# Splitting each weight tile's residual subtraction between VectorE and GpSimd in a one-layer hybrid decoder trunk

## The reference, cut to what matters

```python
h = rmsnorm(x, mix_norm_w[l])
(hq, hf, hi, hg, dq, ..., gz, gate_logits) = jnp.split(h @ w_in[l], IN_SPLITS, axis=-1)
o_a = hgrn2_mixer(...)            # gated linear recurrence
o_b = diff_attention_mixer(...)
o_c = nsa_mixer(...)              # with compress_tokens: flat @ w1
o_d = chunk_gmlp_mixer(...)
merged = sum over b of gates[:, :, b] * (o_b @ w_branch[l, b])
x = x + merged @ w_out[l]
x = x + cross_attention(rmsnorm(x, xa_norm_w[l]), mem_n, xa_w_q[l], xa_w_kv[l], xa_w_o[l])
x = x + swiglu_ffn(rmsnorm(x, ffn_norm_w[l]), ffn_w_in[l], ffn_w_out[l])
return rmsnorm(x, final_norm_w)
```

## Time and profile before

| | |
|---|---|
| Time, median of 3 (lowest to highest) | 2071.66 us (2069.86 to 2072.21) |
| The profiled execution | 2072.21 us, span 2070.4 us |
| PE busy | 2026.4 us, 98% |
| PEld busy | 1772.2 us, 86% |
| DVE busy | 1301.8 us, 63% |
| ACT busy | 936.5 us, 45% |
| POOL busy | 7.9 us, under 1% |
| Granted TensorE clock, mean | 0.995 |

### The profile page before, as it was taken

The page is one execution under the profiler, slowest core; times in us unless marked ns, Lnnn a source line. Parts: engine busy times, 40 slices in busy tenths (PEclk is TensorE's granted clock), DMA queues, the critical chain, the costliest instruction groups (busy, mean ns, idle before and its releaser), DMA issues.

```text
span 2070.4 us, 30081 instructions
## 1 busy us (share of the span) xinstructions
PE 2026.4 (98%) x11734; PEld 1772.2 (86%) x11734; DVE 1301.8 (63%) x1528; ACT 936.5 (45%) x1126; POOL 7.9 (0%) x14
## 2 busy tenths in 40 slices
PE   7999999999999999999999999999999999999997
PEld 6788878887888888888888888888888888888886
DVE  7467776578666656677454447766666666645554
ACT  5364454555444444445434334444444444433342
POOL 0000000000000000000000000000000000000000
PEclk9999999999999999999999999999999999999998
DMA  6444455345555555555555436555555555565553
GB/s 239 143 173 163 172 198 179 133 145 215 189 183 182 183 185 190 214 185 181 194 192 181 144 114 212 203 184 193 191 183 193 191 184 192 191 225 193 192 185 121
DMA packets 53212, 378.29 MB, mean 183 GB/s; under 512 B 6160, under 2 KB 6416, under 8 KB 8464
## 3 DMA queue, kind: packets, MB, share of 16 engines
q1 hardware_dynamic: 50688, 365.71, 50.3%
q10 hardware_dynamic: 2448, 11.48, 1.4%
HBM read 372.98 MB, written 4.19 MB: 182 GB/s over the span
## 4 chain that ended last, share of the span: by engine, by line
PE 55%; issue 36%; DVE 6%; ACT 2%; DMA 0%; POOL 0%; DVEq 0%; POOLq 0%; ACTq 0%
PE acc L1288 33%; PE acc L1289 17%; DVE w_lo L735 2%; PE m L1367 1%; PE m L1696 1%; PE m L1672 1%; ACT w_hi L319 1%; ACT probs L370 0%; DVE x_weighted_split L1044 0%; DVE branch_now L740 0%; DVE norm L779 0%; PE m L1390 0%; DVE branch_gated L1097 0%; PE m L1492 0%; DVE x_split L785 0%
## 5 line engine op out<-in xcount | busy, mean ns | idle before, releaser
L1288 PE MATMUL acc<-x_split,w_hi 128*128 128x512 f32 x3344 | 1179.0, 397 | 10.2 <-DVE x_split L785 6.3
L735 DVE TENSOR_TENSOR w_lo<-raw,w_hi 128x2048 fp32r<-128x2048 f32 x346 | 792.5, 2291 | 351.4 <-ACT w_hi L319 347.3
L1289 PE MATMUL acc<-x_split,w_lo 128*128 128x256 f32 x3344 | 937.7, 280 | 0.0
L1288 PEld LDWEIGHTS acc<-x_split,w_hi 128*128 128x128 f32 x3344 | 628.1, 188 | 156.7 <-DVE x_split L785 6.9
L319 ACT ACTIVATE w_hi<-raw 128x2048 fp32r<-128x2048 f32 x346 | 661.2, 1911 | 99.5 <-DMA raw<-in_w_fo 87.5
L1289 PEld LDWEIGHTS acc<-x_split,w_lo 128*128 128x128 f32 x3344 | 633.0, 189 | 0.5 <-issue 0.2
L329 ACT ACTIVATE evac_half<-acc 128x256 f32<-128x256 f32 x358 | 136.4, 383 | 891.0 <-PE acc L1289 891.0
L1288 PE MATMUL acc<-mem_split,w_hi 128*128 128x512 f32 x768 | 267.9, 393 | 0.7 <-DVE mem_split L1171 0.7
L1288 PE MATMUL acc<-ffn_split,w_hi 128*128 128x512 f32 x704 | 244.1, 391 | 0.0
L1289 PE MATMUL acc<-mem_split,w_lo 128*128 128x256 f32 x768 | 214.9, 280 | 0.0
L1289 PE MATMUL acc<-ffn_split,w_lo 128*128 128x256 f32 x704 | 197.1, 280 | 0.0
(11 more groups left out here) (293 smaller groups left out, 1199.1 us busy)
## 6 DMA issues: line engine op xcount, KB each, us to landing
raw<-in_w_fi SPq DMA_DIRECT2D x88, 1024.0 KB, 4.9
raw<-in_w_gate_b SPq DMA_DIRECT2D x60, 1024.0 KB, 4.9
raw<-in_w_start SPq DMA_DIRECT2D x54, 1024.0 KB, 4.9
raw<-in_w_fo SPq DMA_DIRECT2D x44, 1024.0 KB, 4.9
raw<-in_w_kv SPq DMA_DIRECT2D x32, 1024.0 KB, 4.9
raw<-in_w_gate_a SPq DMA_DIRECT2D x16, 1024.0 KB, 4.9
raw<-in_w_out SPq DMA_DIRECT2D x16, 1024.0 KB, 4.9
raw<-in_w_q SPq DMA_DIRECT2D x16, 1024.0 KB, 4.9
```

The lines of the kernel that those rows point to most:

```text
L735: dve.tensor_tensor(w_lo(n), RAW[:, n[2] % RAWS], w_hi(n).bitcast(F32), ALU.subtract).then_inc(lo_done, 1)
L1288: pe.matmul(acc[bank][:], w_hi(n)[:, c], x, start=start, stop=False)
L1289: return pe.matmul(acc[bank][:, 0:S], w_lo(n)[:, c], x[:, 0:S], start=False, stop=stop)
```

## The change

A tile's subtraction is parted by blocks. DVE does the first `b` of the 16 blocks and POOL the other 16 - `b`, each as one instruction, and PE waits for both. A function picks `b` by the tile's number. Inside loops the tile's number is not known (`None`) and `b` is 10. POOL gets a list of its own, with all 346 tiles and the eight powers between them.

| Tiles | b (DVE) | POOL's blocks |
|---|---|---|
| 0, 1 | 6 | 10 |
| 2 to 5 | 5 | 11 |
| 6 to 15 | 10 | 6 |
| 16 to 35 | 4 | 12 |
| 36 to 53: `cmp` | 8 | 8 |
| 36 to 53: `mix` | 6 | 10 |
| 54 to 69 | 4 | 12 |
| 70 to 74 | 6 | 10 |
| 75 to 345 | 10 | 6 |

```diff
+def dve_blocks(t):
+    if t is not None and t <= 5:
+        return 6 if t < 2 else 5
+    if t is not None and WIDE1 <= t < WIDE1 + 5:
+        return 6
+    if t is None or not WIDE0 <= t < WIDE1:
+        return 10
+    if t < GA0 and START[t][0] == "cmp":
+        return 8
+    return 6 if 36 <= t < GA0 else 4
...
-        lo_done = sem("lo_done")
+        lo_dve = sem("lo_dve")
+        lo_pool = sem("lo_pool")
...
@@ block.gpsimd
+            def lo(n):
+                rs, b = n[2] % RAWS, dve_blocks(tile_no(n))
+                pool.wait_ge(hi_done, val(n, 1))
+                pool.tensor_tensor(w_lo(n)[:, b:TB], RAW[:, rs, b:TB], w_hi(n)[:, b:TB].bitcast(F32),
+                                   ALU.subtract).then_inc(lo_pool, 1)
...
             pool.wait_ge(sem("ones"), 2)
+            lo(at(0))
+            lo(at(1))
             scale("n0", NT)
-            scale("hg", 2 * H)
-            scale("da", 2 * H)
-            for name in ("ln", "nm", "n1", "n2", "n3"):
-                scale(name, NT)
+            for t in range(WIDE1):
+                lo(at(t + AHEAD))
+                if t == 37:
+                    scale("hg", 2 * H)
+                if t == 51:
+                    scale("da", 2 * H)
+                if t == 64:
+                    scale("ln", NT)
+            for t in range(WIDE1, WIDE1 + 4):
+                lo(at(t + AHEAD))
+            steps("gb")
...
+            steps("fi", skip=4)
+            steps("fo", drop=4)
+            for t in range(N_TILES - 4 + AHEAD, N_TILES):
+                lo(at(t))
+            scale("n3", NT)
...
@@ block.vector
             def lo(n):
+                rs, b = n[2] % RAWS, dve_blocks(tile_no(n))
                 dve.wait_ge(hi_done, val(n, 1))
-                dve.tensor_tensor(w_lo(n), RAW[:, n[2] % RAWS], w_hi(n).bitcast(F32), ALU.subtract).then_inc(lo_done, 1)
+                dve.tensor_tensor(w_lo(n)[:, 0:b], RAW[:, rs, 0:b], w_hi(n)[:, 0:b].bitcast(F32),
+                                  ALU.subtract).then_inc(lo_dve, 1)
...
@@ block.tensor
             def tile_ready(n):
-                pe.wait_ge(lo_done, val(n, 1))
+                pe.wait_ge(lo_dve, val(n, 1))
+                pe.wait_ge(lo_pool, val(n, 1))
```

More of the change, by code:

```diff
@@ L230, in known, with tile_no @@
             return n[0] is None
+        def tile_no(n):
+            return n[2] if n[0] is None else None
         def w_hi(n):
@@ L290, in _, with steps @@
             pool.memset(NEGH[:], -0.5).then_inc(sem("ones"), 1)
+            def lo(n):
[3 more added lines that the diff above has]
+                                   ALU.subtract).then_inc(lo_pool, 1)
+            def steps(name, skip=0, drop=0):
+                first, n, _ = PHASES[name]
+                with pool.Fori(0, (n - skip - drop) // 4) as i:
+                    for u in range(4):
+                        lo((i, 4, first + skip + u + AHEAD))
             def scale(name, n):
@@ L297, in _ @@
             pool.wait_ge(sem("ones"), 2)
+            lo(at(0))
+            lo(at(1))
             scale("n0", NT)
-            scale("hg", 2 * H)
-            scale("da", 2 * H)
-            for name in ("ln", "nm", "n1", "n2", "n3"):
-                scale(name, NT)
+            for t in range(WIDE1):
[9 more added lines that the diff above has]
+            steps("gb")
+            first, n, _ = PHASES["wo"]
+            for t in range(first, first + n + 12):
+                lo(at(t + AHEAD))
+                if t == first + 6:
+                    scale("nm", NT)
+                if t == first + n + 3:
+                    scale("n1", NT)
+            steps("kv", skip=12)
+            steps("q")
+            steps("xo")
+            first, _, _ = PHASES["fi"]
+            for t in range(4):
+                lo(at(first + t + AHEAD))
+                if t == 0:
+                    scale("n2", NT)
+            steps("fi", skip=4)
[3 more added lines that the diff above has]
+            scale("n3", NT)
         @block.scalar
```

## The result

| | before | changed |
|---|---|---|
| Time, median of 4 | 2071.93 us | 2141.32 us (2139.03 to 2143.93) |
| Ratio | | 1.0337, 95% interval 1.0320 to 1.0355 |
| Span of the profiled execution | 2070.4 us | 2140.4 us |

A forecast was written before the change was run, and what follows sets the result against it. PE was taken as the bound, so only its stalls outside the feed-forward could be won. Terms of -7.4, -4, -3.4, -0.8 and -0.7 gave -16.3; 2072.2 - 16.3 - 0.5 = 2055.4 us, range 2046 to 2080.

The forecast's parts named there:

- What bounds the kernel: PE, busy 98% of the span; DVE doesn't matter in the 728 us of feed-forward, only stalls elsewhere can be won.
- DVE's share, 0.69 to 1.49 us: DVE's subtraction of 4 to 10 blocks in each tile, priced by columns; saves 1.60 to 0.80 us of DVE.
- nothing takes the place of the gain: Tile 5 path: ACT's copy of w_hi is ready before DVE wants it, so the 6.7 us of shorter subtractions count.
- POOL's share: POOL's subtraction of 6 to 12 blocks: 2.0 to 3.9 us at 2.5 ns a column, hidden within PE's 5.55 us.
- The terms of the sum: Start, tile 5 and clock -7.4, `cmp` tiles -4, `b1` -3.4, `wo` start -0.8, `fi` start -0.7: -16.3 us.
- The rival that I held at 0.21: DVE and POOL instructions with two SBUF inputs hold each other up; +10 to +28 us, likelier +14: 2086; chance 0.21.
- The chances: Odds over the whole kernel's time: faster 0.70, same 0.09, slower 0.21.
- PE's cadence: From 497 to 841 a multiply takes 176.6 ns, in the feed-forward 173.3; a change could take another 6.4 us off.
- the rival with the beat: PE enters `gb` without a stall and loses the slower beat of 497 to 841: 2049 us, chance 0.12.
- The powers' queue: At `hg`, `da` and `ln` powers queue behind POOL's share of tile t+2: costs nothing, or some 2 us each.

The follow-up runs named there:

- the run with fills: Changed kernel, but POOL subtracts only 2 columns of each tile and fills the rest of its blocks with zeros, hardly reading SBUF; 2052.94 us, ratio 0.9901.
- the run of DVE's share alone: Changed kernel, but POOL does nothing for the tiles and PE multiplies w_hi again in place of POOL's blocks; 2045.98 us, ratio 0.9879.
- the run with the powers first: Changed kernel, but POOL does the powers of hg, da and ln before its share of tile t+2, not behind it; 2136.71 us, ratio 1.0326.

## Why the prediction was wrong, point by point

- **What bounds the kernel** held. The feed-forward tiles run without a stall in every kernel (PE is busy for all 560 us from 1420 to 1980 in each profile); the time was lost where DVE sets PE's pace.
- **DVE's share, 0.69 to 1.49 us** held only where POOL doesn't read: 693 and 1493 ns in the run with fills. In the changed kernel the 512-column share took 1710 on average. This is the step that failed, together with "nothing takes the place of the gain". I priced a DVE instruction by its columns and took a second engine's work to be free as long as it fits in PE's 5.55 us a tile. In its place the runs showed that POOL's reading share and a DVE instruction hold each other up for up to a whole instruction: 0.83 us became 3.86, and +69 us came out where I had -16.3.
- **POOL's share** was near: 2.5 ns a column as I put it. From the shortest of 768 and of 1536 columns, 1821 and 3448 ns, it is 2.12 and 190 ns fixed, 3.45 us for the widest share. By the Trainium skill's figure (GPSIMD Engine Reference, Elementwise — side-by-side cycle accounting) it would be about 3.4, an estimate; the trace agrees.
- **The terms of the sum** held without the hold. In the run with fills tile 16 is 7.4 us early (I had 7.4), tiles 36 to 54 bring 3.6 (4), tiles 70 to 80 3.2 (3.4), the start of `wo` 1.5 (0.8), that of `fi` nearly nothing (0.7); PE is idle for 1.6 us from 466 to 482, the `b1` tiles (I had 1.5); the first product starts at 14.74, where I had 15.4. Two microseconds more come between tiles 60 and 66, a stretch where I had forecast nothing. In the run of DVE's share alone tile 16 is 10.6 us early, 3.2 more: the waits for POOL's part, even a filled one, are not free at the start.
- **The rival that I held at 0.21** was right in its mechanism, in its place in steps 1 to 4 (+8.6 predicted, tile 16 is 9.1 late), and in steps 16 to 35 (up to +18, 5.8 found). In steps 1 to 4 the working isn't sound: 3.6 + 0.8 in place of 2.2 is +2.2 and not +1.7, and the share took 3.86 in place of 2.28, +1.6. Its price was far too low, +14 in place of +69: I gave nothing to tiles 36 to 69, which are 42 us late, though the token mixers work from SBUF to SBUF there, on up to 1024 columns. And I left out the half clock that the longer stalls brought with them, some 29 of the 69 us by the estimate above.
- **The chances.** The rule of the Trainium skill (SBUF — State Buffer, Who interferes with whom), by which the second of the two is blocked until the first is done, is what these traces show wherever POOL's share reads beside such an instruction: 0.83 us became 3.86, and pieces of an instruction let the other engine in between. No row of before spoke for or against it, and I treated that as a reason for a low chance. The time at its mechanism's true price would have been outside my range even so.
- **PE's cadence.** In the run of DVE's share alone a multiply takes 173.2 ns from 497 to 798 (1738 in 301 us), in the one with fills 176.5 (1881 in 332), as before. So the rival with the beat, 0.12 of my chances, came about in that one execution. It makes some 6 of the 10 us between these two profiled executions (2042.33 and 2052.29 us); most of the rest is there by tile 70, 17.3 and 13.7 us early. In tiles 16 to 69 alone it is the fast beat as well. The executions of one kernel lie about as far apart (2042.3 and 2049.7 us with DVE's share alone, 2065.0 and 2071.2 to 2073.4 us before), which may be the same beat; only one of each was profiled. Then some 3 of the 25.5 us are the beat. What sets it stays open; it wasn't tried.
- **The powers' queue**, which I had put at nothing, or at some 2 us for each of three powers if that was wrong, stays open between these two: the run with the powers first is 4 to 5 us shorter, within the noise.

## What to carry to other kernels

Before moving elementwise work from DVE to POOL, go through what DVE does at that time and mark each instruction by where its inputs lie. Beside DVE work with an input in PSUM POOL's share was free (2064.5 against 2071.5 us), beside work with two SBUF inputs each side paid up to the other's whole instruction, and a short instruction of a dependent chain paid as much as a long one. If it has to be beside such work, let the long one start behind the short one of the same tile and cut it in pieces: here that took the loss from 69 to 11 us.

## What I had not expected of the hardware

- DVE's `tensor_scalar` with its one tensor input in SBUF is held as well: 128x1024 took 3.79 us at 466.95, beside POOL's share that started at 466.58; a like one at 472.03, with POOL idle, took 0.69. Sixteen of 128x256 took 519 ns on average, 354 before. Not only two-input instructions are at risk.
- Where both engines are released by the same count, DVE was mostly first: in 236 of 281 tiles its 1280-column share started before POOL's and had its bare 1.49 us, and POOL paid (3.15 us as the median of 768 columns, 1.82 alone).
- Size doesn't matter to the held one: an addition of 32x16 values at 29.00 took 3.13 us, 0.16 before.
